# Prompt attention of a hybrid decoder step: masks and maximum in one VectorE pass, small query tiles two pairs ahead

## The reference, cut to what matters

```python
scale = N_HEAD_DIM ** -0.5
s_s = jnp.einsum('bqhgd,bqhsd->bqhgs', q_rot, ks) * scale
p_s = masked_softmax(s_s, (pos_s <= t[None, :, None, None])[:, :, :, None, :])
o_s = jnp.einsum('bqhgs,bqhsd->bqhgd', p_s.astype(q.dtype), vs)
dt = t[:, None] - s_win[None, :]
mask_w = (dt >= 0) & (dt < WINDOW) & (s_win[None, :] >= 0)
s_w = jnp.einsum('bqhgd,bshd->bqhgs', q_rot, kv_win[:, :, 0]) * scale
p_w = masked_softmax(s_w, mask_w[None, :, None, None, :])
o_w = jnp.einsum('bqhgs,bshd->bqhgd', p_w.astype(q.dtype), kv_win[:, :, 1])
return gates[..., 0:1] * o_c + gates[..., 1:2] * o_s + gates[..., 2:3] * o_w
```

## Time and profile before

| what | us |
|---|---|
| median of 3 runs (1068.9 to 1069.88) | 1069.85 |
| the profiled execution | 1074.71 |
| its span, first to last instruction | 1072.9 |
| TensorE busy in the span | 1039.1 (97%) |
| VectorE busy | 474.0 (44%) |
| ScalarE busy | 334.8 (31%) |
| GpSimd busy | 69.3 (6%) |

### The profile page before, as it was taken

How to read it: one execution, slowest core, us unless ns; L and a number is a source line. 1 busy time by engine, 2 the same in 40 slices (tenths; PEclk the granted TensorE clock), 3 DMA queues, 4 the chain that set the end, 5 groups by cost and what they waited for, 6 DMA issues and landing times.

```text
span 1072.9 us, 14761 instructions
## 1 busy us (share of the span) xinstructions
PE 1039.1 (97%) x5449; PEld 629.8 (59%) x5449; DVE 474.0 (44%) x1042; ACT 334.8 (31%) x816; POOL 69.3 (6%) x174
## 2 busy tenths in 40 slices
PE   6999999999999999999999999999999899899997
PEld 6766654444445555588675455666656788445443
DVE  5644451000112222232426887777776456353542
ACT  6321110000001111111104677666766532121121
POOL 1000000000000001112001010100200420000000
PEclk9999999999999999999999999999999999999999
DMA  8402020020403131152102300000020668533512
GB/s 297 206 2 79 0 79 1 14 87 4 78 1 101 20 90 51 35 129 60 52 1 64 94 2 1 2 2 1 8 73 1 167 174 238 162 118 107 169 40 84
DMA packets 83165, 77.49 MB, mean 72 GB/s; under 512 B 28354, under 2 KB 67566, under 8 KB 83030
## 3 DMA queue, kind: packets, MB, share of 16 engines
q1 hardware_dynamic: 71478, 61.82, 19.2%
q10 hardware_dynamic: 11616, 14.74, 4.8%
HBM read 66.59 MB, written 14.10 MB: 75 GB/s over the span
## 4 chain that ended last, share of the span: by engine, by line
PE 89%; DVE 3%; DMA 3%; ACT 2%; issue 2%; SPq 1%; POOL 1%; DVEq 0%; ACTq 0%; POOLq 0%
PE PS L2163 28%; PE PS L2156 16%; PE PS L2405 9%; PE PS L2219 7%; PE PS L2238 6%; PE PS L2251 6%; PE PS L2092 2%; PE PS L1963 1%; PE PS L2078 1%; PE PS L2225 1%; DMA WR<-in_w_out 1%; PE PS L2434 1%; PE PS L1975 1%; DMA out_s_C<-GM 1%; PE PS L2161 1%
## 5 line engine op out<-in xcount | busy, mean ns | idle before, releaser
L2163 PE MATMUL PS<-WR,XT 128*128 128x512 f32 (+1 forms) x768 | 306.9, 557 | 0.0
L2163 PEld LDWEIGHTS PS<-WR,XT 128*128 128x128 f32 x768 | 144.0, 190 | 147.7 <-issue 144.6
L2156 PE MATMUL PS<-XT,WR 128*128 128x352 f32 x576 | 172.7, 460 | 0.0
L2156 PEld LDWEIGHTS PS<-XT,WR 128*128 128x128 f32 x576 | 108.5, 190 | 58.9 <-issue 0.4
L1635 DVE TENSOR_REDUCE XT<-PS 128x1 f32<-128x640 f32 (+7 forms) x128 | 84.4, 701 | 27.7 <-PE PS L2225 27.2
L2219 PE MATMUL PS<-KTR,XT 64*128 64x512 f32 (+3 forms) x352 | 79.1, 507 | 0.4 <-ACT XT L1189 0.2
L1189 ACT ACTIVATE XT<-PS,XT 128x640 f32<-128x640 f32 (+7 forms) x96 | 66.8, 702 | 8.7 <-DVE XT L1635 8.6
L2238 PE MATMUL PS<-cst,XT 128*128 128x128 f32 x396 | 62.3, 281 | 4.3 <-DVE XT L1646 3.2
L2405 PE MATMUL PS<-WR,KT 128*128 128x512 f32 x128 | 61.7, 604 | 2.0 <-DMA WR<-in_w_out 2.0
L2405 PE MATMUL PS<-WR,QT 128*128 128x512 f32 x128 | 61.2, 599 | 0.0
L1646 DVE TENSOR_SCALAR XT<-XT,small 128x640 f32<-128x640 f32 (+7 forms) x96 | 53.8, 560 | 3.5
(11 more groups left out here) (470 smaller groups left out, 1226.4 us busy)
## 6 DMA issues: line engine op xcount, KB each, us to landing
WR<-in_w_in SPq DMA_DIRECT2D x24, 512.0 KB, 8.0
WR<-in_cache_kv_cmp SPq DMA_DIRECT2D x56, 128.0 KB, 2.5
MT<-row_factors ACTq DMA_DIRECT2D x16, 256.0 KB, 7.2
WR<-in_w_in SPq DMA_DIRECT2D x32, 128.0 KB, 3.2
QN<-in_cache_kv_win SPq DMA_DIRECT2D x8, 512.0 KB, 5.9
out_s_kv_win<-in_cache_kv_win SPq DMA_DIRECT2D x1, 4064.0 KB
out_y_prompt<-MT ACTq DMA_DIRECT2D x7, 512.0 KB, 2.9
XT<-in_x_prompt ACTq DMA_DIRECT2D x6, 512.0 KB, 4.2
```

Source lines behind the costliest of these rows:

```text
L2156: ins = mm(b[:, 0:THIRD], w[:, k, r // 3 * P:(r // 3 + 1) * P], xt[:, k, r % 3 * THIRD:(r % 3 + 1) * THIRD], **f)
L2163: ins = mm(b[:, 0:width], xt[:, k, r * P:(r + 1) * P], w[:, k, :], **f)
```

## The change

Four things change together.

- The mask matmuls go (the two in `scores`). The masks lie in SBUF instead, as a table `mask_blocks` of 16 blocks of 128 columns in fp32, built once by GpSimd in the key columns of KVN, which are free once the keys are turned and stored. `mask_of` picks the nb blocks that a pair needs.
- `max_of` becomes one `tensor_tensor_reduce`: it reads the scores in PSUM and the mask blocks in SBUF, writes -(score + mask) to SBUF where the weights will be, and keeps the minimum, which is the negated maximum. The exponential then runs in place in SBUF, with scale -1. The scores of a later pair wait for `s_max` instead of `s_exp`, and the wait for the weight buffer (`p_turned`) moves from ScalarE's `exps` to VectorE's `max_of`.
- For pairs of at most 4 blocks the weight buffers are halves of 512 columns, so four pairs have room (`weights`), and scores and maxima run two pairs ahead (`scored_by`). Larger pairs stay one ahead.
- In the same small pairs ScalarE does both exponentials of p + 1 before it takes the turned weights of (p, 0).

The core of the diff:

```diff
+        mask_blocks = KVN[:, :].rearrange("p (n c) -> p n c", n=2 * NT)[:, :, 0:P]
...
+        def weights(p, h):
+            nb = pair(p)[4]
+            c = p // 2 % 2 * 512 if nb <= 4 else 0
+            return pp[p % 2][h][:, c:c + nb * P]
+        def mask_of(p):
+            i, br, g, k0, nb = pair(p)
+            n = 8 if br and i >= WB else 8 - nb
+            return mask_blocks[:, n:n + nb, :]
+        def scored_by(p):
+            return min(p + 2 if p + 2 < NT * PAIRS and pair(p + 2)[4] <= 4 else p + 1, NT * PAIRS - 1)
...
@@ GpSimd, behind the rotation of tile 0
+                if i == 0:
+                    pool.wait_ge(kt_turned, 4)
+                    pool.wait_ge(stored_rot, (NT + WB) * 16)
+                    link(nc.gpsimd.memset(mask_blocks[:, 0:13, :], 0.0))
+                    for n, c in ((7, K_CAUSAL), (8, K_OLD), (12, K_CAUSAL)):
+                        ins = nc.gpsimd.tensor_copy(mask_blocks[:, n, :], masks[:, c:c + P])
+                    ins.then_inc(blocks_zeroed, 1)
...
@@ ScalarE
-                if p >= 2:
-                    act.wait_ge(p_turned, turn_count[u - 3])
-                nc.scalar.activation(pp[p % 2][h][:, 0:nb * P], bank(score_bank(p, h), -(-nb // 4))[:, 0:nb * P], ACT.Exp,
+                nc.scalar.activation(weights(p, h), weights(p, h), ACT.Exp, scale=-1.0,
...
-                take_turned(p, 0)
+                early = p + 1 < NT * PAIRS and pair(p + 1)[4] <= 4
+                if not early:
+                    take_turned(p, 0)
                 if p + 1 < NT * PAIRS:
                     for h in range(KVH):
                         exps(p + 1, h)
+                if early:
+                    take_turned(p, 0)
                 take_turned(p, 1)
...
@@ VectorE
-                nc.vector.tensor_reduce(nmax[:, u % 4:u % 4 + 1], bank(score_bank(p, h), -(-nb // 4))[:, 0:nb * P], AX.X, ALU.max,
-                                        negate=True).then_inc(s_max, 1)
+                back = 4 if nb <= 4 else 2
+                if p >= back:
+                    dve.wait_ge(p_turned, turn_count[u - 2 * back + 1])
+                by_block = lambda x: x.rearrange("p (n t) -> p n t", t=P)
+                nc.vector.tensor_tensor_reduce(by_block(weights(p, h)), by_block(bank(score_bank(p, h), -(-nb // 4))[:, 0:nb * P]),
+                                               mask_of(p), -1.0, 3e38, ALU.add, ALU.min, nmax[:, u % 4:u % 4 + 1]).then_inc(s_max, 1)
...
+            dve.wait_ge(blocks_zeroed, 2)
+            for p in range(2):
+                for h in range(KVH):
+                    max_of(p, h)
...
-                        max_of(p + 1, h)
+                    for n in range(scored_by(p - 1) + 1 if p else 2, scored_by(p) + 1):
+                        for h in range(KVH):
+                            max_of(n, h)
...
@@ TensorE
-                            pe.wait_ge(s_exp, 2 * p - 1 + h)
+                            pe.wait_ge(s_max, 2 * p - 1 + h)
...
-                            pe.wait_ge(s_exp, 2 * p - 3 + h)
+                            pe.wait_ge(s_max, 2 * p - 3 + h)
...
-                    if old:
-                        mm(bank(2 * h)[:, 0:P], idb, masks[:, K_OLD:K_OLD + P], start=False, stop=nb > 4)
-                    last = nb - 1
-                    mm(bank(score_bank(p, h) + last // 4)[:, last % 4 * P:(last % 4 + 1) * P], idb, masks[:, K_CAUSAL:K_CAUSAL + P],
-                       start=False, stop=True).then_inc(s_done, 1)
...
+            scores(1)
             for p in range(NT * PAIRS):
                 i = p // PAIRS
-                if p + 1 < NT * PAIRS:
-                    scores(p + 1)
+                for n in range(scored_by(p - 1) + 1 if p else 2, scored_by(p) + 1):
+                    scores(n)
```

More of the change, by code:

```diff
@@ L1654, in take_outputs @@
                                         ALU.mult).then_inc(on_ready, 1)
-            for h in range(KVH):
-                max_of(0, h)
+            dve.wait_ge(blocks_zeroed, 2)
+            for p in range(2):
+                for h in range(KVH):
+                    max_of(p, h)
             for h in range(KVH):
@@ L2208, in scores @@
                     pe.wait_ge(qz_ready, i + 1)
-                old = br == 1 and i >= WB
                 for j in range(0, nb, 4):
@@ L2237, in turn_weights @@
                     for k in range(n):
-                        ins = nc.tensor.transpose(bank(4 + y % 2)[:, k * P:(k + 1) * P], pp[p % 2][h][:, (j + k) * P:(j + k + 1) * P], ident)
+                        ins = nc.tensor.transpose(bank(4 + y % 2)[:, k * P:(k + 1) * P], weights(p, h)[:, (j + k) * P:(j + k + 1) * P], ident)
                     ins.then_inc(p_turned, 1)
@@ L2283, in _ @@
             id32 = ident[0:NS, 0:NS]
-            pe.wait_ge(s_exp, NT * PAIRS * 2)
+            pe.wait_ge(s_max, NT * PAIRS * 2)
             def turn_sample(q, chs=range(4)):
```

13 lines of the change are left out of this document (7 added, 6 removed).

## The result

| | before | changed | ratio, 95% interval |
|---|---|---|---|
| median of 4 runs each, us | 1069.87 (1068.9 to 1070.9) | 1057.37 (1056.59 to 1059.87) | 0.9872 [0.9852, 0.9892] |
| profiled execution, us | 1074.71 | 1056.59 | |
| its span, us | 1072.9 | 1054.8 | |
| mean granted clock | 0.992 | 0.993 | |

The change makes the kernel 1.3% faster: 12.5 us by the medians, 18.1 us by the two profiled executions.

What follows compares the result with a forecast made beforehand. TensorE was taken to bound query tiles 3 to 7, VectorE tiles 0 to 2 after the change. Gains 5.2 + 7.3 + 3.7 less 0.7 and 0.4 make 15.1 us, so 1055 us, own range 1052 to 1059.

Steps and rivals of the forecast that it cites:

- The scores wait for the maximum: Query tiles 4 to 7: scores wait for VectorE's maximum, not ScalarE's exponential; 7.3 us gained, 3.7 least, 9 most.
- Mask matmuls: Removing TensorE's mask matmuls gains 4.5 us in tiles 4 to 7 and 0.7 in tile 3, together 5.2 us.
- The slack of the turn: Eight-block pair: scaled weights are ready 0.8 us before TensorE's turn asks for them, 0.4 us after the read-outs.
- The pass: VectorE's two-source pass replacing each of 128 reductions costs the same as the reduction, 0.69 us on 512 columns.
- The read-out: Second VectorE instruction reading the accumulator after each pass: 0.205 us each, 16 per tile, 3.3 us a tile.
- Tiles 0 to 3: Working two pairs ahead makes VectorE the bound; gains 2.6, 0.1, 1.0 and, in tile 3, none beyond masks: 3.7 us.
- The start and the tail: Costs at the ends: first scale behind pair 1's passes, 0.7 us; last pair's two uncovered read-outs, 0.4 us.
- From the span to the median: The span's 15.1 us difference was taken off the 1069.85 us median, 4.9 below the profiled execution, giving 1054.8 us.
- the short read-out: Rival, chance 0.18: each read-out takes 0.11 us and tiles 0 to 2 gain more, 1050 us.
- The long read-out: Rival, chance 0.13: each read-out takes 0.4 us, tiles 0 to 3 lose 7.7 us, 1067 us.
- the half rate: Rival, chance 0.08: VectorE's pass takes twice the time per column, making the kernel slower, 1107 us.
- the moved wait: Rival, chance 0.11: turns wait for scaled weights instead of scores for banks, the 7.3 us come back, 1062 us.

## Why the prediction was right

The forecast was 1055 us; 1057.37 and 1053.21 were measured, on both sides of it. The difference it worked out, 15.1 us, stands against 17.3 in the windows at full clock.

- **The scores wait for the maximum: right, and undersized.** 7.3 us forecast in tiles 4 to 7; 7.5 measured with the masks in, 9.1 with them out, the top of my range. The 1.38 us in window 3 were not in the sum.
- **Mask matmuls: right in kind, 5.2 against 4.0** in windows 3 to 7 (3.6 in 4 to 7, where I had 4.5). The cut accounts for a little: the scores of three pairs of tile 4 lie ahead of window 4. What I gave back for a turn that no longer stands behind masks, 0.04 a pair, is there: the turns take 1.3 us more over 29 pairs. What I had at nothing are the three turns that now wait for their scaled weights, 0.5 us. The masks also stood in the way in windows 1 and 2 (0.9), where I had costed them at nothing. For tiles 4 to 7 the two steps and the tail make 11.4 forecast, 11.1 measured: the errors cancel.
- **The slack of the turn: right but for three turns.** I gave it 0.8 us, 0.4 after the read-outs, and no wait. In the pair shown the scaled weights are ready 0.75 us before the load. The list has eight waits of 5.3 us, against 1.0 us before, and I had named such waits as what would make me wrong; by the starts of the matmuls they cost 0.5 us.
- **The pass: right.** 688 ns on 512 columns against 0.69 forecast. The Trainium skill (Vector Engine (DVE) Microarchitecture Reference, Points that are easy to get wrong) says that an instruction family with an accumulator runs at half the throughput with two non-bf16 sources in SBUF. In this kernel's pass, with one source in PSUM, there is no halving; no run here has both in SBUF.
- **The read-out: the step that failed, though the number held.** I took 0.205 us each, 3.3 us a tile. The row says 83 ns, and all of that lies in the edge of the next pass: two passes and read-outs took 2.37 us where two reductions took 2.35. Net it adds at most 9 ns at 512 columns. By the Trainium skill (VectorE: DVE Perf Modes, the section on the trn2 errata), 58 cycles and the elements, one column is 61 ns, an estimate that is nearer to the row than my 0.205 us.
- **Tiles 0 to 3: undersized, and not for that reason alone.** 3.7 us forecast for tiles 0 to 2, 0.7 for tile 3 and 0.7 lost at the start, 3.7 in all; windows 0 to 3 gave 6.2. The cut of the changed kernel stands two passes later in windows 0 to 2. With those passes moved to where they stood (0.84, 1.11 and 1.38 us by the rows of 2, 3 and 4 blocks; an estimate), tiles 0 to 3 gave 2.1, 1.3, 0.9 and 1.9 against 1.9, 0.1, 1.0 and 0.7. VectorE's busy share in window 1 is 89%, not over 90, and its busy time did not grow by the 3.3 us that were to fill the tile. The start and the tail were not measured by themselves. Nor is the read-out the whole of it: a linked instruction of 209 ns behind each pass took 6.5 us, as much as windows 0 to 3 had gained, where my sum with that price still had 3.7. So two errors met, and the bound by VectorE's busy time is too simple; what else the depth gives there is open.
- **From the span to the median: the weak place.** I took the difference off a median 4.9 us below the profile and called the clock in tile 0 a matter of 1 to 2 us in one rival. The clock moves window 0 by 2.05 (before) and 2.57 us (changed), and two medians of the changed kernel lie 4.2 us apart. That 1055 falls between them is in part luck.

Of the rivals, the short read-out has the mechanism; its sum without its extras was 18.6 us, against the measured 17.3. The long read-out and the half rate are excluded by their rows, and the moved wait came with 0.5 of its 7.3 us. (The sum of the long read-out has a slip: 16 times 0.4 is 6.4, not 6.6, which would make it 0.8 us less.) GpSimd's mask table is hidden: it is done at 559.2 us, and the first pass starts at 572.55.
